# First feed-forward projection as seven block products with weight sums made in DRAM

## What is computed

```python
h = rms_norm(x, g_mix)                       # then q, k, v of two attentions and two gates: h @ w_in
x = x + merged @ w_out                       # merged: gated sum of the two attentions' outputs
h2 = rms_norm(x, g_ffn)
x = x + jnp.square(jax.nn.relu(h2 @ w_ff1)) @ w_ff2     # w_ff1 1024 x 4096, w_ff2 4096 x 1024
```

## Time and profile before

| | |
|---|---|
| three runs | 676.51, 676.52, 677.76 us; median 676.52 |
| the profiled execution | 675.73 us, span of the profile 673.9 us |
| busy share of the span | PE 99%, weight loads 82%, DVE 75%, ACT 55%, POOL 48% |
| moved by DMA | 69.87 MB, mean 104 GB/s |
| matmuls | 3238 |

### The profile page before, as it was taken

How to read it: one execution, slowest core, us unless ns; L and a number is a source line. 1 busy time by engine, 2 the same in 40 slices (tenths; PEclk the granted TensorE clock), 3 DMA queues, 4 the chain that set the end, 5 groups by cost and what they waited for, 6 DMA issues and landing times.

```text
span 673.9 us, 9473 instructions
## 1 busy us (share of the span) xinstructions
PE 667.9 (99%) x3238; PEld 553.5 (82%) x3238; DVE 504.3 (75%) x701; ACT 370.4 (55%) x662; POOL 322.6 (48%) x194
## 2 busy tenths in 40 slices
PE   9999999999999999999999999999999999999997
PEld 8877788888888888888888888888888888888886
DVE  6677898655555555875559879787897888979797
ACT  7467677776666566544357546253553625536360
POOL 0246676466555652444445536246452444436432
PEclk9999999999999999999999999999999999999999
DMA  8322242222332113555222322315132151230303
GB/s 321 104 85 94 82 132 72 80 79 95 94 94 94 65 46 116 164 177 185 80 79 93 121 98 80 137 62 177 51 112 96 62 187 62 93 113 13 125 0 125
DMA packets 22910, 69.87 MB, mean 104 GB/s; under 512 B 2732, under 2 KB 4012, under 8 KB 22877
## 3 DMA queue, kind: packets, MB, share of 16 engines
q1 hardware_dynamic: 22588, 68.92, 30.6%
q10 hardware_dynamic: 288, 0.52, 0.2%
HBM read 67.27 MB, written 2.16 MB: 103 GB/s over the span
## 4 chain that ended last, share of the span: by engine, by line
PE 96%; DVE 1%; ACT 1%; DMA 1%; POOL 0%; issue 0%; SPq 0%; DVEq 0%; ACTq 0%
PE bank L1379 21%; PE bank L1381 21%; PE bank L1380 20%; PE bank L1699 8%; PE bank L1696 8%; PE bank L1698 8%; PE bank L1480 3%; PE bank L1529 2%; PE bank L1545 2%; PE bank L1566 1%; PE bank L1568 1%; DMA store<-x_t 1%; PE bank L1668 1%; DVE store L1014 0%; PE bank L1407 0%; PE bank L1408 0%
## 5 line engine op out<-in xcount | busy, mean ns | idle before, releaser
L538 POOL TENSOR_TENSOR w_lo<-w_raw,w_hi 128x1024 fp32r<-128x1024 f32 x77 | 190.5, 2478 | 233.1 <-ACT w_hi L628 233.1
L1379 PE MATMUL bank<-qk_hi,w_hi 128*128 128x512 f32 x320 | 125.0, 391 | 0.0
L1381 PE MATMUL bank<-qk_hi,w_lo 128*128 128x512 f32 x320 | 124.5, 389 | 0.0
L1380 PE MATMUL bank<-qk_lo,w_hi 128*128 128x512 f32 x320 | 124.5, 389 | 0.0
L1379 PE MATMUL bank<-x_hi,w_hi 128*128 128x512 f32 x304 | 122.5, 403 | 1.2 <-DVE v_parts L1020 1.1
L1381 PE MATMUL bank<-x_hi,w_lo 128*128 128x512 f32 x304 | 118.9, 391 | 0.0
L1380 PE MATMUL bank<-x_lo,w_hi 128*128 128x512 f32 x304 | 118.4, 390 | 0.0
L628 ACT ACTIVATE w_hi<-w_raw 128x1024 fp32r<-128x1024 f32 x80 | 83.9, 1057 | 58.8 <-PE bank L1381 55.1
L1262 DVE SCALAR_TENSOR_TENSOR store<-bank,softmax,store 128x512 f32<-128x512 f32 x101 | 71.9, 743 | 23.0 <-PE bank L1699 22.9
L1699 PE MATMUL bank<-v_parts,x_lo 128*128 128x512 f32 (+1 forms) x218 | 84.4, 387 | 0.0
L1696 PE MATMUL bank<-v_parts,x_hi 128*128 128x512 f32 (+1 forms) x218 | 84.4, 387 | 0.0
(11 more groups left out here) (165 smaller groups left out, 1211.7 us busy)
## 6 DMA issues: line engine op xcount, KB each, us to landing
w_raw<-slabs SPq DMA_DIRECT2D x80, 512.0 KB, 3.3
bias_m<-slabs SPq DMA_DIRECT2D x16, 512.0 KB, 3.6
qk_hi_again<-slabs SPq DMA_DIRECT2D x16, 512.0 KB, 5.1
store<-x_t SPq DMA_DIRECT2D x16, 256.0 KB, 3.3
bias_m<-tab_dram SPq DMA_DIRECT2D x8, 256.0 KB, 4.3
out<-store SPq DMA_DIRECT2D x7, 256.0 KB, 2.8
bias_m<-tab_dram SPq DMA_DIRECT2D x8, 128.0 KB, 3.7
w_raw<-slabs ACTq DMA_DIRECT2D x2, 256.0 KB, 3.3
```

Of the source, the lines that this page charges most:

```text
L538: pool.tensor_tensor(w_lo[:, g % WS, :], w_raw[:, g % RAW, :], w_hi[:, g % WS, :].bitcast(F32), ALU.subtract).then_inc(w_lo_ready, 1)
L1379: pe.matmul(out_, wh, xh, start=first, stop=False)
L1380: pe.matmul(out_, wh, xl, start=False, stop=False)
L1381: last = pe.matmul(out_, wl, xh, start=False, stop=end)
```

## The change

Chunk 0 keeps its four slabs. In chunks 1 to 7 h2 @ w_ff1 too is done with seven block products (`up(k, c)`, U0 to U6 below). A product is 2 x 4 x 3 = 24 matmuls of 256 columns, 168 in a chunk, on banks 7 and 6 only: U2 accumulates on U0's bank, U3 and U5 on U1's, U6 on U4's.

- The four sums of x blocks are made once, during the output slabs, by DVE (`half_sums`, `half_sum_lo`) and ACT (`scaled_x1`, `half_sum_hi`), into `sum_hi` and `store_low`.
- The four sums of w_ff1 blocks of a chunk are made in DRAM: ACT issues 28 plain copies DRAM to DRAM (`copy_sum`), POOL 28 adding DMAs onto them (`add_to_sum`, `accum_op=ALU.add`) during projections, attention, branch and output slabs.
- Low parts of the weights of U0 to U3: ACT writes the negated high part over the raw weights (`up_minus`), and an adding DMA from POOL adds the raw weights from DRAM to it (`up_add`). Those of U4 to U6 are POOL subtractions as before.
- DVE adds the products' banks to the u blocks in SBUF (`up_product`, five a chunk); ACT copies U0's bank (`first_up_copy`).
- Down products run in the order 0, 2, 1, 3, 4, 5, 6; the low part of unit 4 moves from DVE to POOL. Queues of SP and POOL are unrolled instead of looping.

The core of the diff, queue by queue (`c` is the chunk):

```diff
+UPS = 7
+RAW_SLOT, HIGH_SLOT = [0, 1, 2, 3, 4, 5, 0], [0, 1, 2, 3, 0, 1, 2]
+ADDED_UPS = 4
+UP_BANK = [7, 6, 7, 6, 7, 6, 7]
+UP_OPENS = (0, 1, 4)
+ORDER, LAST_ORDER = [0, 2, 1, 3, 4, 5, 6], [0, 1, 2, 3, 4, 5, 6]
-T_UNITS, B_UNITS = (1, 2, 4, 6), (0, 3, 5)
+T_UNITS, B_UNITS = (1, 2, 6), (0, 3, 4, 5)
...
 PE
+            def up(k, c):
+                if k < ADDED_UPS:
+                    pe.wait_ge(up_added[k], c * 16)
+                else:
+                    pe.wait_ge(up_lo_ready, c * (UPS - ADDED_UPS) + (k - UPS + 1))
+                if k == 0:
+                    pe.wait_ge(up_read, c * UP_READS)
+                elif k == 2:
+                    pe.wait_ge(first_up_copied, c)
+                elif k == 4:
+                    pe.wait_ge(relu_ready, c * TILES + 1)
+                elif k >= 3:
+                    pe.wait_ge(up_read, c * UP_READS + {3: 1, 5: 2, 6: 3}[k])
...
+                for n in range(2):
+                    for i in range(KT // 2):
...
+            ups(b)
+            for k in ORDER[:5]:
                 product(k, b)
+            ups(c)
+            for k in ORDER[5:]:
                 product(k, b)
...
 DVE
+            def up_product(k, c):
+                to = up_from[k]
+                dve.wait_ge(up_done, up_count(k, c))
...
+                dve.tensor_tensor(to, halves(bank[UP_BANK[k]][:, :]), with_, ALU.add).then_inc(up_read, 1)
...
+            def chunk_start(c):
+                weight_sum_1(c)
+                weight_sum_2(c)
+                down_lo(1, c)
+                up_product(1, c)
+                down_lo(2, c)
+                weight_sum_3(c)
+                weight_sum_4(c)
+                up_product(3, c)
+                u_part_lo(6, c)
+                up_product(4, c)
+                up_product(5, c)
+                u_part_lo(0, c)
+                u_sum_1(c)
+                up_product(6, c)
+                u_sum_2(c)
+                u_part_lo(2, c)
+                u_part_lo(1, c)
+                add_both(0, c)
+                u_sum_3(c)
+                u_part_lo(3, c)
+                u_sum_4(c)
+                u_part_lo(4, c)
+                add_both(2, c)
+                add_both(1, c)
+                u_part_lo(5, c)
+                add_both(3, c)
+                down_lo(6, c)
+                add_both(4, c)
...
 DVE, last chunk
             weight_sum_1(c)
+            up_product(1, c)
             weight_sum_2(c)
             weight_sum_3(c)
+            for m in range(2):
+                scaled(1, m, common[m], rest_sum_ready)
+            up_product(3, c)
...
 POOL
+            def up_add(k, c):
...
+                pool.wait_ge(up_minus_ready, (c - 1) * ADDED_UPS + k + 1)
+                pool.dma_start(w_low[:, k, :], src, accum_op=ALU.add).then_inc(up_added[k], 16)
...
             def chunk_lows(c):
                 down_lo(0, c)
+                if c:
+                    up_lo(4, c)
+                    up_lo(5, c)
+                down_lo(3, c)
+                if c:
+                    up_lo(6, c)
+                down_lo(4, c)
+                if c == CHUNKS - 2:
+                    for k in range(ADDED_UPS):
+                        up_add(k, c + 1)
+                    down_lo(5, c)
+                else:
+                    up_add(0, c + 1)
+                    down_lo(5, c)
+                    for k in range(1, ADDED_UPS):
+                        up_add(k, c + 1)
...
 ACT
+            def next_splits(c):
+                down_hi(4, c)
...
+                    up_split(0, c + 1)
+                    down_hi(5, c)
+                    down_hi(6, c)
+                    for k in range(1, ADDED_UPS):
+                        up_split(k, c + 1)
...
+            def chunk(c):
+                down_hi(0, c)
+                down_hi(1, c)
+                first_up_copy(c)
+                up_hi(4, c)
+                down_hi(2, c)
+                up_hi(5, c)
+                down_hi(3, c)
+                up_relu(0, c)
+                up_square(0, c)
+                up_hi(6, c)
+                u_part_hi(6, c)
...
 SP
+            for c in range(CHUNKS):
+                if c:
+                    sp.wait_ge(up_done, up_count(0, c))
+                    load_up(6, c)
+                if c and c + 1 < CHUNKS:
+                    for k in (1, 2, 3, 4, 5):
+                        sp.wait_ge(up_done, up_count(k, c))
+                        load_up(k, c + 1)
+                    sp.wait_ge(up_done, up_count(6, c))
+                    load_up(0, c + 1)
...
-    nc = bacc.Bacc("TRN2", target_bir_lowering=False, num_devices=1)
+    nc = bacc.Bacc("TRN2", target_bir_lowering=False, num_devices=1, dynamic_dma_scratch_size=2048)
```

More of the change, by code:

```diff
@@ L452, in load_down @@
                 sp.dma_start(raw_b[b], src).then_inc(b_arrived[b], 16)
[L454 to L461 removed]
+            for g in range(2, G_FF + TILES):
                 if g == 16:
@@ L508, in _ @@
-            with sp.Fori(0, CHUNKS - 2) as c:
-                loads(c, range(AHEAD, AHEAD + TILES))
-            loads(CHUNKS - 2, [AHEAD])
+                load_down(b, slabs[G_DOWN + (c + 1) * TILES + b])
+            sp.wait_ge(w_lo_ready, G_FF + TILES - 1)
+            for k in range(RAW):
+                load_up(k, 1)
+            sp.wait_ge(slab_done, G_FF + TILES)
+            for k in range(RAW, UPS - 1):
+                load_up(k, 1)
+            for c in range(CHUNKS):
[8 more added lines that the diff above has]
+                    load_up(0, c + 1)
+                if c + 1 < CHUNKS:
+                    reload(B11, product_done, product_count(2, 1, c), c)
+                    reload(B12, product_done, product_count(4, 1, c), c)
+                    reload(B22, b_lo_ready, c * len(B_UNITS) + len(B_UNITS), c)
+                    reload(B21, t_lo_ready, c * len(T_UNITS) + len(T_UNITS), c)
@@ L614, in last_lows @@
                 down_lo(5, c)
-            with pool.Fori(0, CHUNKS - 1) as c:
+            for c in range(CHUNKS - 1):
                 chunk_lows(c)
@@ L816, in _ @@
                     x1_rows_copy(n - 1)
[L818 to L826 removed]
+                    scaled_x1(n - 1)
+                if n in (3, 5, 7):
+                    half_sum_hi((n - 3) // 2)
@@ L910, in last_chunk @@
                 down_hi(6, c)
-            relu(0, 0)
+            relu(0)
             split_hi(G_FF + 2)
-            square(0, 0)
+            square(0)
             x1_rows_copy(KT - 1)
-            chunk(0, first=True)
-            with act.Fori(1, CHUNKS - 1) as c:
+            scaled_x1(KT - 1)
+            first_chunk(0)
+            with act.Fori(1, CHUNKS - 2) as c:
                 chunk(c)
+            chunk(CHUNKS - 2)
             last_chunk(CHUNKS - 1)
@@ L1690, in product_part, with ups @@
+            def ups(c):
+                for k in range(UPS):
+                    up(k, c)
             def product_part(k, m, out_, high, low, cols, opens):
```

499 lines of the change are left out of this document (335 added, 164 removed).

## The result

The changed kernel takes 708.38 us (706.77 to 709.79, 4 runs) where the kernel before takes 676.51 beside it: ratio 1.0469 [1.0452, 1.0487], slower. The profiled execution has a span of 706.6 us against 673.9, +32.7.

A forecast was written before the change was run, and what follows sets the result against it. PE, busy 99%, was taken to bound the kernel, with every added wait paid in full. Chunks 1 to 6 +20, chunk 7 +6 and attention +1 gave +27 on 676.5, so 703.5 us, range 666 to 716.

The forecast's parts named there:

- 256 columns at 0.120 us: PE's up products: 168 matmuls of 256 columns take 20.16 us against 21.76, 1.60 us less a chunk.
- The chain to U5: Chunks 1 to 6: DVE and POOL passes take turns, U3's addition ends at 18.3, U5 starts 3.9 us late.
- The tail ahead of P4 and P5: Down products, chunks 1 to 6: PE waits for POOL's low parts, +0.2 us at P4 and +0.7 at P5.
- Chunks 1 to 5 in all: Feed-forward chunks 1 to 5: 44.1 us a chunk against 40.8, +3.3 each, +16.5 together.
- Lateness of U1 to U4 lies under the wait for U5: Chunks 1 to 6: lateness of U1 to U4 up to 4 us, as from adding DMAs, costs nothing extra.
- The sign of 3 to 4 us idle ahead of U5: Sign of being right, chunks 1 to 6: PE idle 3 to 4 us ahead of U5, released by DVE's bank addition.
- Chunk 0 at nothing: Chunk 0, which keeps its four slabs: change of 0 us.
- Chunk 7 +6: Last chunk: late addition of U3 and U0's wait for an adding DMA, +6 us, ends -1.6 and +10.
- Attention +1: Attention: POOL's issuing of adding DMAs, mostly hidden, costs +1 us, ends 0 and +4.
- DVE is what has no room: DVE's chunk budget: 43.1 us where PE needs 39.2, so DVE cannot fit its work.
- the rival in which everything fits: POOL's passes fall clear of DVE's weight sums, only -11.2 us stays, 665.3 us; chance 0.22 with its neighbours.
- The budget of DVE: DVE per chunk: 27.9 us bare, 8.7 waiting for POOL and 6.5 idle, 43.1 in all.

The follow-up runs named there:

- The run that only writes: Changed kernel with the DMAs that make the low parts of U0 to U3's weights writing instead of adding; 711.02 us, ratio 1.0516.
- later half sums: Changed kernel with DVE's last half sums of x and one low part in chunk 0 moved behind the u blocks' low parts; 703.73 us, ratio 1.0398.
- the third order: Changed kernel with ACT, POOL and DVE queues reordered, among others U0's bank copied before unit 1's high part; 682.12 us, ratio 1.0086 to the kernel before.

## Why the prediction was right, and where it was not

The forecast was 703.5 us, range 666 to 716; measured 708.38. Step by step:

- **256 columns at 0.120 us: right.** An up product takes 2.88 us where nothing waits and the clock is up, and a chunk without waits 39.5 for the worked 39.2.
- **The chain to U5: right.** From U0 (481.81): POOL's pass for U4 ends at 9.4 (forecast 9.3), DVE's low part of unit 2 at 10.5 (10.5), POOL's for U5 at 12.7 (12.9), weight sum 3 at 13.8 (14.05), POOL's for unit 3 at 16.1 (16.45), weight sum 4 at 17.1 (17.6), U3's addition at 17.75 (18.3), P0 at 23.65 (24.2). The tail ahead of P4 and P5 was 0.3 and 0.45 (0.2 and 0.7). Chunks 2 to 5 lost 2.7 to 3.0 each (3.3).
- **Chunks 1 to 5 in all, 16.1 for 16.5: in part luck.** Chunk 1 lost 5.0, by a late load that reached U2 through DVE and ACT and by the lower clock behind it. Neither was in the forecast; they fill the gap that the other four left.
- **"Lateness of U1 to U4 lies under the wait for U5": right in the sum, wrong in the picture.** The adding DMAs land in 7.5 and about 10 us, above the bound of 3.3 to 6.6, and so U1 and U3 wait, which the forecast had named as a sign against itself. U5's wait is shorter by as much. The sign of 3 to 4 us idle ahead of U5 was not met (1.6 at most). The run that only writes shows the cover: with these waits gone U5's went to 2.8. The cover is not whole (0.8 us a chunk was saved in waiting), and the lower clock behind the longer wait cost more than that.
- **Chunk 0 at nothing: the step that failed**, 6.4 us, more than the whole difference of 4.9 between forecast and result. Three things were missed: the moved slab was P0's cover (argued from PE's two orders and from the row above, by which P0's low part was 2.3 us later than P0 would have been due; the 0.9 us that P0 still waits with later half sums agree, a run with the slab put back was not made); DVE's half sums, put down as 0 to 1 in the output slabs, stand partly in chunk 0 and take turns there; and a standstill of 3.6 us costs more than itself, for the clock fell: 1.6 us here, about as much again in chunk 1 and in chunk 7. The forecast left the clock out.
- **Chunk 7 +6: right in size.** Chunks 6 and 7 together +8.7 (9.3), of which 1.4 is the lower clock; U0 waited 2.1 us for its adding DMA, as foreseen, and U6 2.5 for DVE.
- **Attention +1:** not shown; the stretch varies by 2 us, and without those DMAs the time is the same.
- **"DVE is what has no room", and the turns come "whoever goes first": wrong as a reason.** That was said against the rival in which everything fits. The same passes fit into 39.5 to 39.8 us in the third order, in which the addition that PE waits for stands ahead of a pass that could wait. The loss of the changed kernel in chunks 1 to 5 is its order: 220.1 us, 198.5 at best. Had the change come with that order, the rival would have been nearly right for five chunks of eight (5.5 us saved there of the 8.0 worked). The budget of DVE went wrong where it carried the 8.7 us of waiting for POOL over as a constant: by its own 27.9 us of bare work, the 37.6 busy of the changed kernel hold 9.7 of waiting, the 33.7 of the third order 5.8. And DVE was busy 87% of that stretch in the changed kernel, not over 90%.

What stays open: whether chunk 0 and chunk 7, which keep 4.0 and 2.4 us (87.7 against 85.3) over the kernel before, can be ordered as well; every move tried there brought the wait back at a later product.

## What to carry to other kernels

Work out, for each result that the bound engine waits for, what stands ahead of it in its producer's queue, and let the bank additions and copies go before any pass that is needed later; with two queues that lock each other out, such a pass costs its own time and the other's (3.4 us for 1.2). Judge a wait by taking it away: two waits in a row can cover one another, and a moved pass can bring its wait back two products on. Read the granted clock behind every wait of 2 us or more: here the lower clock cost 1.5 us behind some of them, and in one run it hid a small gain. When a change moves work in a queue, ask what the moved work had covered.
